# First feed-forward part in seven block products instead of eight, and the modulation rows moved from VectorE to GpSimd and ScalarE

## Chip, cores and metric

One core of a Trainium2 chip. The metric is the time on the device in microseconds, of one execution of the whole program; the median of three runs before the change is 2452.07 us (2451.47 to 2453.34).

## The reference

Two layers over 1024 latent tokens of width 1024. Layer 0 mixes tokens by attention, layer 1 by a short gated convolution, and each is followed by a SwiGLU feed-forward part with 2816 inner features. Every sub-layer is normalized, then scaled and shifted, and its result is gated, with six vectors a layer that come from silu(c) times `ada_w`:

```python
sh1, sc1, g1, sh2, sc2, g2 = jnp.split((silu_c @ ada_w[i] + ada_b[i])[:, None, :], 6, axis=-1)
...
x = x + g1 * y
x = x + g2 * swiglu(modulate(rmsnorm(x, norm_ffn[i]), sh2, sc2), ffn_w_gate[i], ffn_w_up[i], ffn_w_down[i])

def swiglu(h, w_gate, w_up, w_down):
    return (jax.nn.silu(h @ w_gate) * (h @ w_up)) @ w_down
```

All is float32. The output is the latent stream after a last RMSNorm.

## The kernel before

**Precision.** A float32 operand is held as two fp32r parts, a high one (`_hi`) that ScalarE rounds and a low one (`_lo`) that VectorE makes by subtraction. A product of two such operands is three matmuls (`mm3`: hi.hi, hi.lo, lo.hi; lines 571 to 573), each 128x128 by 128x512.

**Layout.** `x` and `h` lie transposed: 8 chunks of 128 features by 1024 tokens, the tokens in two halves A and B of 512. PSUM has 8 banks of 512: 0 to 3 for gate and up, 4 to 7 for the down product.

**Stages.** Prologue, attention, output projection, f0 (feed-forward of layer 0), the convolution, f1 (feed-forward of layer 1), last norm. Each engine's program is written out by hand in order; engines meet at semaphores (`wait_ge`, `then_inc`), and an instruction that waits holds all that stands behind it on its engine. SP issues all loads, in one queue.

**f0 before.** 11 blocks of 2x128 inner features (`ffn`, `inner`). A block is four units of gate and up (8 chunks x 2 x 3 = 48 matmuls each) and a down product for each half (8 x 2 x 3 = 48 each): 288 matmuls. Weight tiles (128x1024) go through `raw` and are split into `w_hi`, `w_lo`; `t_lo` counts tiles whose low part is made, and a tile's load waits until the tile two before it has been split. `to_x` adds a down bank, times the gate vector, to `x`; PE may fill the bank again once that is done (`bank_free`).

**Modulation rows before.** The 48 columns of layer 1's vectors are 48 rows of `ada_w`: each is loaded (128x1024, `modf_in`), multiplied by `row_f` (silu(c)) and summed along the row by one VectorE instruction (`mod_row_f`, L2256), five rows a block, from two buffers. `modf_c` counts them. After the last, `mods` and the scale vectors of layer 1 are made.

**f1 before.** Block 0 as in f0; the other ten (s = 0 to 9, `WINO`) by seven block products in place of eight. Both W^T and h are cut 2x2 (two tiles by two halves of the 8 chunks; two halves of the chunks by two halves of the tokens): A11, A12, A21, A22 of the weights, and sums S1 to S4; B11, B21, B22 and T1 to T4 of h, made once (`b_part`, `b_top`, `b_low`). A product has 4 chunks x 3 = 12 matmuls, 7 products for each of gate and up: 168, and 96 of the down products: 264 a block. Operands go through rings of four (`op_hi`, `op_lo`): ACT's `operand_top` n waits for product n - 4, VectorE's `operand_low` follows. VectorE adds the products up out of PSUM (`part`: C11, U2, U3, U5, C22, C21, C12); ACT takes silu of a corner's gate (`corner_gate`), VectorE multiplies (`corner_mult`), ACT rounds (`corner_split`), VectorE makes the low part (`corner_low`, counted by `gl`). The down product of half A runs one block late, behind products A11 and A12 of GATE; that of B later in the block. `quad_in` loads a block's four gate and up tiles into `rq`, line 747 its two down tiles into `w_lo_f`, copied by `down_top` and `down_low`.

**At the seams.** The norm of a half is: squares by ACT, sums by POOL (L2679), column sum by PE (`job_sum`), root by ACT (`job_sqrt`), reciprocal and diagonal by VectorE (`job_diag`), broadcast by PE (`job_bcast`), copy `rstd` by ACT (`job_out`). Then `h_scaled`, `h_top_of`, `h_low` make h chunk by chunk (`h_chunks`), with `to_x` of the other half between.

## Time and profile before

| | |
|---|---|
| median of three runs | 2452.07 us |
| the profiled execution | 2453.06 us, its span 2451.7 us |
| mean granted TensorE clock | 0.990 |
| PE busy | 2397.5 us (98%), 11229 matmuls |
| DVE, ACT, POOL busy | 1507.0, 711.8, 150.1 us |
| the chain that ended last | PE 93% of it, DVE 4% |

PE is TensorE's matmuls, PEld its weight loads, DVE VectorE, ACT ScalarE, POOL GpSimd, SP the queue that issues loads. Times are from the span's start. f0 lies between about 655 and 1385 us, the convolution up to 1746, f1 up to 2426. A matmul in the timeline has about 0.39 us because matmuls are pipelined; what counts is from start to start. "Idle before" is the time in which the engine did nothing, "releaser" what ended it. The granted clock is a share of 2.4 GHz.

### The profile page before, as it was taken

To read this page: it belongs to the slowest core of one execution; us is meant where nothing else is said; L and a number is where in the kernel's file an instruction comes from. 1 tells how busy PE (TensorE), PEld (TensorE's weight loads), DVE (VectorE), ACT (ScalarE), POOL (GpSimd) and SP (SyncE) were. 2 spreads that over 40 slices of the span, in tenths; PEclk is the share of its full clock that TensorE was granted. 3 is DMA by queue.
4 is the path that set the end of the run, shared out by engine and by line. 5 is a ranking of instruction groups with operands and counts; after the bars stand their busy time and mean duration, and the time that the engine had idled before them with its cause. 6 is when DMAs were issued, how large, how long until landed. Compare 5 with 4: busy or idle time off the path is not lost.

```text
span 2451.7 us, 28775 instructions
## 1 busy us (share of the span) xinstructions
PE 2397.5 (98%) x11229; PEld 1977.7 (81%) x11229; DVE 1507.0 (61%) x2204; ACT 711.8 (29%) x1105; POOL 150.1 (6%) x109
## 2 busy tenths in 40 slices
PE   7999999999999999999999999999999999999997
PEld 4878888888788888888888788888778888888886
DVE  4667777786665444454443763553887777777775
ACT  5345545553421111011111421111532222222223
POOL 0111121100300000000000300000300000000002
PEclk9999999999999999999999999999999999999998
DMA  7101111123222222222211111111101111111102
GB/s 285 33 24 42 50 49 41 41 78 116 91 95 79 93 86 86 95 89 83 93 63 51 59 53 32 64 44 42 52 9 53 59 52 52 52 52 56 56 27 86
DMA packets 48050, 163.31 MB, mean 67 GB/s; under 512 B 5184, under 2 KB 6592, under 8 KB 47808
## 3 DMA queue, kind: packets, MB, share of 16 engines
q1 hardware_dynamic: 47936, 161.72, 20.1%
q8 instruction: 80, 1.31, 0.2%
q14 instruction: 34, 0.28, 0.0%
HBM read 157.51 MB, written 4.19 MB: 66 GB/s over the span
## 4 chain that ended last, share of the span: by engine, by line
PE 93%; DVE 4%; ACT 1%; DMA 1%; issue 1%; POOL 0%; SPq 0%; ACTq 0%; DVEq 0%; POOLq 0%
PE ps L571 26%; PE ps L573 26%; PE ps L572 26%; PE ps L993 3%; PE ps L927 2%; PE ps L931 1%; PE ps L929 1%; PE ps L928 1%; PE ps L932 1%; PE ps L972 1%; PE ps L974 1%; PE ps L973 1%; DVE h_lo L2221 1%; DVE x L2000 1%; DMA ada_ring<-ada_pe 1%; PE ps L1015 1%
## 5 line engine op out<-in xcount | busy, mean ns | idle before, releaser
L571 PE MATMUL ps<-h_hi,w_hi 128*128 128x512 f32 x1152 | 451.7, 392 | 11.3 <-DVE h_lo L2221 11.2
L572 PE MATMUL ps<-h_lo,w_hi 128*128 128x512 f32 x1152 | 449.4, 390 | 0.0
L573 PE MATMUL ps<-h_hi,w_lo 128*128 128x512 f32 x1152 | 449.3, 390 | 0.0
L2000 DVE SCALAR_TENSOR_TENSOR x<-ps,mods,x 128x512 f32<-128x512 f32 x448 | 327.9, 748 | 140.0 <-PE ps L573 119.8
L571 PE MATMUL ps<-g_hi,w_hi 128*128 128x512 f32 x832 | 325.2, 391 | 3.4 <-DVE x L2000 1.8
L572 PE MATMUL ps<-g_lo,w_hi 128*128 128x512 f32 x832 | 323.8, 389 | 0.0
L573 PE MATMUL ps<-g_hi,w_lo 128*128 128x512 f32 x832 | 323.7, 389 | 0.0
L571 PEld LDWEIGHTS ps<-h_hi,w_hi 128*128 128x128 f32 x1152 | 216.9, 188 | 61.0 <-DVE h_lo L2221 16.6
L573 PEld LDWEIGHTS ps<-h_hi,w_lo 128*128 128x128 f32 x1152 | 217.0, 188 | 45.4
L572 PEld LDWEIGHTS ps<-h_lo,w_hi 128*128 128x128 f32 x1152 | 217.0, 188 | 44.4
L2241 DVE TENSOR_TENSOR ab<-ab,ps 128x512 f32<-128x512 f32 x48 | 33.0, 687 | 312.6 <-PE ps L573 307.5
L2679 POOL TENSOR_TENSOR acc<-acc,sq 128x512 f32<-128x512 f32 x52 | 75.4, 1450 | 1876.0 <-ACT sq L1324 1873.4
L571 PEld LDWEIGHTS ps<-g_hi,w_hi 128*128 128x128 f32 x832 | 156.2, 188 | 39.0 <-DVE x L2000 3.8
L573 PEld LDWEIGHTS ps<-g_hi,w_lo 128*128 128x128 f32 x832 | 156.2, 188 | 32.6
L572 PEld LDWEIGHTS ps<-g_lo,w_hi 128*128 128x128 f32 x832 | 156.2, 188 | 31.9
L1344 ACT CAST w_hi<-raw 128x1024 fp32r<-128x1024 f32 x112 | 113.6, 1050 | 197.4 <-PE ps L573 156.5
L1567 ACT ACTIVATE ab<-ps 128x512 f32<-128x512 f32 x48 | 28.7, 598 | 489.8 <-PE ps L573 489.7
L1854 DVE TENSOR_TENSOR pt_lo<-ps,pt_hi 128x512 fp32r<-128x512 f32 x160 | 110.1, 689 | 72.3 <-ACT pt_hi L1412 71.7
L1634 ACT CAST op_hi<-rq 128x512 fp32r<-128x512 f32 x120 | 73.5, 621 | 237.6 <-PE ps L573 236.4
L1854 DVE TENSOR_TENSOR w_lo<-raw,w_hi 128x1024 fp32r<-128x1024 f32 x108 | 131.0, 1229 | 16.5 <-ACT w_hi L1344 16.3
L1412 ACT CAST pt_hi<-ps 128x512 fp32r<-128x512 f32 x160 | 93.8, 587 | 131.6 <-PE ps L993 131.6
L571 PE MATMUL ps<-h_hi,op_hi 128*128 128x512 f32 x320 | 125.1, 391 | 2.0 <-DVE w_lo L1854 2.0
(336 smaller groups left out, 4030.4 us busy)
## 6 DMA issues: line engine op xcount, KB each, us to landing
raw<-stream SPq DMA_DIRECT2D x112, 512.0 KB, 3.6
mod_raw_f<-ada_rows SPq DMA_DIRECT2D x48, 512.0 KB, 3.7
rq<-stream SPq DMA_DIRECT2D x40, 512.0 KB, 3.5
mod_raw<-ada_rows SPq DMA_DIRECT2D x32, 512.0 KB, 3.5
w_lo_f<-stream SPq DMA_DIRECT2D x20, 512.0 KB, 4.0
ada_ring<-ada_pe SPq DMA_DIRECT2D x16, 512.0 KB, 11.0
x<-x_t SPq DMA_DIRECT2D x8, 512.0 KB, 7.2
out_t<-x SPq DMA_DIRECT2D x16, 256.0 KB, 2.1
```

Of the source, the lines that this page charges most:

```text
L571: nc.tensor.matmul(out, w[0][wi], a[0][ai], start=start, stop=False)
L572: nc.tensor.matmul(out, w[0][wi], a[1][ai], start=False, stop=False)
L573: return nc.tensor.matmul(out, w[1][wi], a[0][ai], start=False, stop=stop)
L927: nc.tensor.matmul(dst, qa[par][0][:, q], ckv_hi[:, k0:k1], start=True, stop=False)
L993: last = nc.tensor.transpose(ps[:, bank, j * P:(j + 1) * P], pbuf[:, 4 * (gb % 2) + j, k * P:(k + 1) * P], ident[:])
L1344: copy(dst, raw[k][:]).then_inc(t_hi, 1)
L1412: copy(pt_hi[:, (10 * gb + k) % 4, :], ps[:, bank, :]).then_inc(ra, 1)
L1634: copy(op_hi[:, at % 4, :], operand_a(s, mat, name)).then_inc(op_h, 1)
L1854: return nc.vector.tensor_tensor(dst, full, hi.bitcast(F32), ALU.subtract)
L2000: nc.vector.scalar_tensor_tensor(out=x[:, m, HALF[half]], in0=ps[:, out_bank(d, m), :], scalar=mods[:, gate + m:gate + m + 1], in1=x[:, m, ...
L2241: nc.vector.tensor_tensor(ab[unit % 2][:], ab[unit % 2][:], ps[:, 2 * (unit % 2) + 1, :], ALU.mult)\
L2679: nc.gpsimd.tensor_tensor(acc_of(j)[:, 0:cols], acc_of(j)[:, 0:cols], sq[C.n["sqa"] % 2][:, 0:cols], ALU.add).then_inc(sqa, 1)
```

## The change

- f0 runs as f1 does: block 0 as before, then ten blocks s = 0 to 9 of seven products; f1's are now s = 10 to 19. All helpers take s for both parts (`at_first`, `at_end`: first and tenth of a part).
- The last block of each part (`at_end`) has another order of products (A22 ahead of S1), and its own down products are cut in two (`down_end`): first the corner that is ready, then the other. The norm of half A (`job_sum`, `job_bcast`) comes before and inside the last down product.
- Corners are now put together in `g_full`, which shares the memory of `g_hi` and `g_lo`; so C11 and C22 are read after the last `to_x` of a down product and not before it. `ab` is free, and in f0 `mod_raw_f` lies there, one buffer.
- The modulation rows: SP loads a row when ACT has summed the one before it, POOL multiplies it by `row_f`, ACT sums it (`row_sum`). Blocks s = 0 to 5 of f0 take five rows, 6 to 8 take six. The scale vectors of layer 1 are made after block 8.
- The convolution's first tiles are loaded after f0's last block, and the start of the convolution stands in `conv_start`.

The rows' places, and SP (loads):

```diff
+ROWS_OF = {s: range(5 * s, 5 * s + 5) if s < 6 else range(6 * s - 6, 6 * s) for s in range(WINO - 1)}
...
-            if n >= 2:
-                sp.wait_ge(modf_c, n - 1)
-            sp.dma_start(mod_raw_f[n % 2][:], ada_rows[N_ATT_MOD + n]).then_inc(in_modf[n % 2], 16)
+            if n:
+                sp.wait_ge(modf_c, n)
+            else:
+                sp.wait_ge(gl, GL_F0 + 4)
+            sp.dma_start(mod_raw_f[:], ada_rows[N_ATT_MOD + n]).then_inc(in_modf, 16)
...
+        def down_in(s):
+
+            at = f0_at if s < WINO else f1_at
+            sp.wait_ge(dn, 8 * (down_at(s) + 2))
+            for f in range(2):
+                sp.dma_start(w_lo_f[:, 4 + f, :], stream[at(6 * (s % WINO + 1) + 4 + f)]).then_inc(in_dn[f], 16)
...
+        def wino_in(s):
+
+            rows = list(ROWS_OF.get(s, ()))
+            for n in rows[1:4]:
+            if at_end(s):
+                down_in(s)
+                return
+            for mat in (GATE, UP):
+                sp.wait_ge(op_l, product_n(s, mat, "A22") + 1)
+                quad_in(s + 1, mat, 1)
+            for n in rows[4:5]:
                 modf_in(n)
+            sp.wait_ge(op_l, product_n(s, GATE, "S4") + 1)
+            quad_in(s + 1, GATE, 0)
+            for n in rows[5:]:
+                modf_in(n)
+            down_in(s)
+            sp.wait_ge(op_l, product_n(s, UP, "S4") + 1)
+            quad_in(s + 1, UP, 0)
+            for n in ROWS_OF.get(s + 1, ())[:1]:
+                modf_in(n)
+
+        stream_in(12, 14)
+        sp.wait_ge(dn, 8 * D_F0)
+        sp.wait_ge(t_lo, 14)
+        quads_first(0)
+        modf_in(0)
+        for s in range(WINO):
+            wino_in(s)
+        sp.wait_ge(op_l, product_n(WINO - 1, GATE, "S4") + 1)
+        stream_in(14, len(TILES))
```

PE (products and the end of a part's last block):

```diff
+        def down_end(s, d, half, corners, norm_job=None):
+
+            for at, corner in enumerate(corners):
+                f = CORNER_F[corner]
+                pe.wait_ge(gl, corner_gl(s, corner))
+                for m in range(4):
+                    if at == 0:
+                        bank_free(d, m)
+                    last = mm3(ps[:, 4 + m, :], (w_hi, w_lo), (ALL, 4 + f, slice(m * P, (m + 1) * P)),
+                               (g_hi, g_lo), (ALL, f, HALF[half]), at == 0, at == 1)
+                    if at == 1:
+                        last.then_inc(dn, 1)
+                if at == 0 and norm_job is not None:
                     job_bcast(norm_job)
+            for m in range(4, KD):
+                bank_free(d, m)
+                for f in range(2):
+                    last = mm3(ps[:, 4 + m % 4, :], (w_hi, w_lo), (ALL, 4 + f, slice(m * P, (m + 1) * P)),
+                               (g_hi, g_lo), (ALL, f, HALF[half]), f == 0, f == 1)
+                last.then_inc(dn, 1)
...
+            products(s, (UP, "A11"), (UP, "A12"), (GATE, "S2"), (GATE, "S3"))
+            if at_end(s):
+                pe.wait_ge(gl, corner_gl(s - 1, "C12"))
+                down_of(d_was + 1, B)
+                products(s, (UP, "S2"), (UP, "S3"), (GATE, "A22"), (UP, "A22"), (GATE, "S1"))
+                pe.wait_ge(dn_l, 2 * s + 2)
+                down_end(s, d_was + 2, A, ("C11", "C21"))
+                products(s, (UP, "S1"), (GATE, "S4"))
+                job_sum(job_a)
+                products(s, (UP, "S4"))
+                down_end(s, d_was + 3, B, ("C22", "C12"), job_a)
+                return
+            products(s, (UP, "S2"), (UP, "S3"), (GATE, "S1"))
+            if not at_first(s):
```

ACT:

```diff
+        def row_sum(s, n):
+
+            for row in ROWS_OF.get(s, ())[n:n + 1]:
+                act.wait_ge(modf_p, row + 1)
+                nc.scalar.activation(mod_raw_f[:], mod_raw_f[:], ACT.Identity,
+                                     accum_out=mods[:, 48 + row:49 + row]).then_inc(modf_c, 1)
...
+                return
+            row_sum(s, 1)
+            for n in range(8, 11):
                 operand_top(s, n)
+            row_sum(s, 2)
+            operand_top(s, 11)
+            operand_top(s, 12)
+            row_sum(s, 3)
             corner_gate(s, "C22")
             operand_top(s, 13)
             corner_split(s, "C22")
-            if s < WINO - 1:
-                operand_top(s + 1, 0)
+            operand_top(s + 1, 0)
+            row_sum(s, 4)
             corner_gate(s, "C21")
             for f in range(2):
                 down_top(s, f)
             corner_split(s, "C21")
-            if s < WINO - 1:
-                operand_top(s + 1, 1)
+            operand_top(s + 1, 1)
+            row_sum(s, 5)
             corner_gate(s, "C12")
+        def wino_end(s, jobs_a):
+
+            for n in range(8, 12):
+                operand_top(s, n)
...
+            corner_gate(s, "C21")
+            operand_top(s, 12)
+            corner_split(s, "C21")
+            operand_top(s, 13)
+            corner_gate(s, "C22")
+            for m in range(KD):
+                squares_of(jobs_a, down_at(s) + 2, m)
+            corner_split(s, "C22")
+            corner_gate(s, "C12")
+            job_sqrt(jobs_a)
+            if s < WINO:
+                top("conv", 0, "c", 0, (prod, product_n(s, UP, "S2") + 1))
+                top("conv", 0, "x", 0, (prod, product_n(s, UP, "S2") + 1))
+            corner_split(s, "C12")
+            job_out(jobs_a)
...
+        def conv_start(turn, jobs_b):
+
+            d = down_at(WINO - 1) + 3
+            free = (prod, product_n(WINO - 1, UP, "S1") + 1)
+            top("conv", 0, "b", 0, free)
+            for k in range(KD):
+                h_top_of(turn, A, k)
+                if k >= 2:
+                    squares_of(jobs_b, d, k - 2)
+            for m in (6, 7):
+                squares_of(jobs_b, d, m)
+            for name in "cxb":
+                top("conv", 0, name, 1, free)
```

VectorE (the reads of C11 and C22 move behind the updates of x), and POOL:

```diff
-            part(s, "C11", GATE)
             for m in range(4):
                 to_x(d_was, m, gate)
...
             for m in range(4, KD):
                 to_x(d_was, m, gate)
...
+            part(s, "C11", GATE)
...
+            for s in range(s0, s0 + WINO):
+                wino_block(s, gate, job_a)
+                if s == WINO - 2:
+                    dve.wait_ge(modf_c, N_F0_MOD)
+                    own(nc.vector.tensor_tensor(mods[:, 48:96], mods[:, 48:96], adab[:, 48:96], ALU.add))
+                    scale_vec(3, mods[:, mod_col(1, SCALE1):mod_col(1, SCALE1) + KD], 2).then_inc(sv_set, 1)
+                    scale_vec(4, mods[:, mod_col(1, SCALE2):mod_col(1, SCALE2) + KD], 3).then_inc(sv_set, 1)
+
+        def conv_start(turn, gate):
+
+            d = down_at(WINO - 1) + 3
+            dve.wait_ge(sv_set, 3)
+            for f, name in ((0, "c"), (0, "x")):
+                low("conv", 0, name, f)
+            for k in range(KD):
+                h_chunks(turn, A, k, k + 1)
+                to_x(d, k, gate)
+                if k == 0:
+                    low("conv", 0, "b", 0)
+            for name in "cxb":
+                low("conv", 0, name, 1)
...
         squares_sum(J_MIX)
         squares_sum(J_MIX + 1)
+        pool.wait_ge(silu_done, 3)
+        for n in range(N_F0_MOD):
+            pool.wait_ge(in_modf, 16 * (n + 1))
+            nc.gpsimd.tensor_tensor(mod_raw_f[:], mod_raw_f[:], row_f[:], ALU.mult).then_inc(modf_p, 1)
```

## Rows read from the trace of the kernel before

**Rows 1.** Busy time of each engine over the span (the page's first part)
```profile
PE 2397.5 (98%) x11229; PEld 1977.7 (81%) x11229; DVE 1507.0 (61%) x2204; ACT 711.8 (29%) x1105; POOL 150.1 (6%) x109
```

**Rows 2.** Windows of the span (start:end, length, each engine's busy us (instructions), clock, DMA)
```profile
1086.22:1151.50 65.28, 65.28 (x289) 54.07 (x288) 31.14 (x44) 8.40 (x11) 0.00 (x0) 1.00 0.28 89
2049.14:2109.00 59.86, 59.86 (x266) 49.56 (x265) 42.41 (x63) 16.32 (x27) 0.00 (x0) 1.00 0.17 53
1869.63:2389.14 519.51, 519.51 (x2293) 430.18 (x2292) 365.77 (x536) 137.91 (x221) 0.00 (x0) 1.00 0.15 49
```

**Rows 3.** Waits over the whole span (engine line <- waited for: total us, times, longest)
```profile
PE ps L571 <- DVE h_lo L2221: 11.2, 9, 2.0
PE ps L1299 <- POOL acc L2679: 3.8, 1, 3.8
```

**Rows 4.** What touches mod_raw_f (durations min/median/max in ns), and where its loads land
```profile
L2256 DVE SCALAR_TENSOR_TENSOR mod_raw_f<-mod_raw_f,row_f x48: 1215/1218/1226, 705.3 to 1274.4; 128x1024 f32<-128x1024 f32 x48
DMA to landing us min/median/max: 3.3/3.7/4.9
```

**Rows 5.** The adds of line L2679 (durations min/median/max in ns)
```profile
L2679 POOL TENSOR_TENSOR acc<-acc,sq x52: 1277/1303/2381, 630.9 to 2428.7; 128x512 f32<-128x512 f32 x52
```

**Rows 6.** Groups by shape on ACT (busy us, mean ns | idle before)
```profile
L1449 ACT ACTIVATION_READ_ACCUMULATOR pbuf<-ps,nmax 128x1 f32 x64 | 12.7, 198 | 0.0
```

**Rows 7.** Timeline around a block of f1 (start, length, ..., [idle before <- releaser])
```profile
2051.64 1.40 DVE L2000 SCALAR_TENSOR_TENSOR x<-ps,mods,x 128x512 f32<-128x512 f32 x2
...
2090.14 0.80 SPq L747 DMA_DIRECT2D w_lo_f<-stream  x2
2095.64 0.62 ACT L1634 CAST op_hi<-rq 128x512 fp32r<-128x512 f32 x1 [0.70 <-PE ps L573]
2097.47 1.99 ACT L1663 CAST w_hi<-w_lo_f 128x1024 fp32r<-128x1024 f32 x2
2101.38 1.22 DVE L1854 TENSOR_TENSOR w_lo<-w_lo_f,w_hi 128x1024 fp32r<-128x1024 f32 x1
2103.11 0.68 DVE L2409 TENSOR_TENSOR ab<-part_ug,ps 128x512 f32<-128x512 f32 x1
```

**Rows 8.** Timeline of POOL and DVE where the convolution begins
```profile
1383.51 4.08 POOL L2679 TENSOR_TENSOR acc<-acc,sq 128x512 f32<-128x512 f32 x2 [16.92 <-ACT sq L1324]
...
1383.99 0.75 DVE L2221 SCALAR_TENSOR_TENSOR h_lo<-tmp,mods,h_hi 128x512 fp32r<-128x512 f32 x1
1384.65 0.75 DVE L2000 SCALAR_TENSOR_TENSOR x<-ps,mods,x 128x512 f32<-128x512 f32 x1
1386.36 1.78 DVE L2221 SCALAR_TENSOR_TENSOR h_lo<-tmp,mods,h_hi 128x512 fp32r<-128x512 f32 x1
1388.06 0.74 DVE L2000 SCALAR_TENSOR_TENSOR x<-ps,mods,x 128x512 f32<-128x512 f32 x1
```

**Rows 9.** Line L747, the loads of down tiles in f1
```profile
DMA to landing us min/median/max: 3.4/4.0/4.7
```

**Rows 10.** Timeline of PE, matmuls with idle time before them
```profile
721.61 0.50 PE L571 MATMUL ps<-g_hi,w_hi 128*128 128x512 f32 x1 [0.69 <-DVE x L2000]
...
1393.54 0.80 PE L571 MATMUL ps<-h_hi,w_hi 128*128 128x512 f32 x1 [2.03 <-DVE h_lo L2221]
...
1752.89 0.50 PE L571 MATMUL ps<-h_hi,w_hi 128*128 128x512 f32 x1 [1.71 <-DVE h_lo L2221]
...
1805.12 0.47 PE L571 MATMUL ps<-g_hi,w_hi 128*128 128x512 f32 x1 [1.10 <-issue]
...
1826.44 0.47 PE L571 MATMUL ps<-h_hi,op_hi 128*128 128x512 f32 x1 [2.02 <-DVE w_lo L1854]
```

**Rows 11.** A window in f1's first product block
```profile
1826.80:1830.20 3.40, 3.40 (x10) 2.62 (x9) 3.40 (x6) 0.00 (x0) 0.00 (x0) 0.50 0.01 2
```

**Rows 12.** Timeline of PE behind its last wide matmul
```profile
2430.30 1.30 PE L1299 MATMUL ps<-ones,acc 128*128 128x1 f32 x8 [3.75 <-POOL acc L2679]
2431.46 3.55 PE L1299 MATMUL ps<-ones,tmp 128*128 128x1 f32 x16
```

590 lines of the change are left out of this document (239 added, 351 removed).

## The prediction, as it stood before the change was run

> **What bounds the kernel now.** I read the page first: TensorE (PE) is busy 2397.5 of 2451.7 us, VectorE (DVE) 61%, ScalarE (ACT) 29%, GpSimd (POOL) 6% [rows 1]. Then the busy time by windows: a block of the first feed-forward part (f0) takes 65.28 us and a seven-product block of the second part (f1) 59.86 us, both with PE busy in every microsecond and the clock at 1.00 (2.4 GHz) [rows 2]. f0 has 288 matmuls of 512 columns in a block and f1 264 (the counts in the rows take in one or two at the edges), so both run at 65.28/288 = 59.86/264 = 0.2267 us each. So the matmul count sets the time, and anything else costs only where PE stands still. The waits of PE over the whole span are few: 11.2 us for h_lo (the three places where a part begins) and 3.8 us for POOL at the end [rows 3]. So I ask of each step of the change: does PE wait for it?
>
> **The change, part by part.**
>
> 1. Fewer matmuls. In ten blocks of f0 gate and up take 2 x 7 products x 4 x 3 = 168 instead of 192. 240 x 0.2267 = 54.4 us less. All of it is on the path.
>
> 2. The 48 multiply-and-sum steps (1.22 us each, 58 us with their accumulator reads left out) leave DVE [rows 4]. The f1 block has 42.4 us of DVE work in 59.86 us [rows 2], none of it late, and f0 now gets the same. Worth nothing by itself.
>
> 3. Each of the 48 rows is now one chain on a single buffer: SP loads it from HBM, POOL multiplies 128x1024, ACT sums it, SP loads the next. No row shows the multiply. POOL's adds of 128x512 have a median of 1.30 us and a maximum of 2.38 [rows 5], so it lies between 1.3 and 4.8; I take 2 x 1.30 = 2.6, since both inputs double. ACT: 0.20 us for the accumulator [rows 6] plus 1.05 for 1024 elements (two such copies, overlapping a little, take 1.99 [rows 7]) = 1.25. A row's load takes 3.7 us [rows 4]. A chain is then 3.7 + 2.6 + 1.25 + about 0.3 = 7.9 us, and five or six of them (39 or 47 us) fit in a block. In the middle of a block this hides: ACT works 16.3 us of a block's 59.86 [rows 2], and operands are copied three products (8 us) ahead.
>
> 4. What POOL does to DVE. While POOL adds, DVE operations with two SBUF inputs wait for it: h_lo (L2221) takes 0.75 us in one place and 1.78 in another, and the update of x (L2000), with one input in PSUM, stays at 0.74 [rows 8]. So one 2.6 us multiply can hold DVE for 2.6 us. By the Trainium skill (SBUF — State Buffer, Who interferes with whom) such an instruction and a GpSimd one that reads SBUF take turns and the second blocks fully; the trace agrees with 1.78 against 0.75 us [rows 8]. By the rule the whole 2.6 us of a multiply counts, as in my sum; if only the 1.03 us seen here were ever held, steps 4 to 6 would come to some 6 us less.
>
>    Where is DVE's critical stretch? At the end of a block DVE must finish the low parts of C21, of the second down tile and of an operand before it reads C12 (2103.11 to 2103.79), which frees the bank that product A12 of the next block wants 2.72 us after the block starts at 2103.56, at 2106.28 [rows 7]: 2.5 us of cover. For blocks 0 to 5 the fifth row's sum falls behind the operand copy at 2095.64, so the next block's first row is loaded from 2097.6, lands at 2101.2 and is multiplied until 2104. It holds DVE by about 2.6 us: PE waits 0.1 to 0.2 us. 6 x 0.2 = 1.2 us (0 to 6).
>
> 5. The sixth row in blocks 6, 7 and 8. SP issues it *before* the two down tiles, and its load waits for the fifth sum. Now the down tiles go out at 2090.14 [rows 7]; then they go at about 2098.0 and 2098.4, behind the row's load. A load lands 3.5 us after its issue, and one right behind another up to 4.7 [rows 9], some 1.3 us more each. They land at 2102.5 and 2103.8. ACT, which copies them in its queue ahead of the C21 cast and the operand, is through at 2104.8 instead of 2099.5, C21's cast at 2105.4, then DVE: low of C21 2106.1, of the tile 2107.3, of the operand 2107.9, C12 2108.5. PE starts A12 at 2108.7 instead of 2106.3: 2.4 us. DVE is now 5.4 us late. Its first update of x (2051.64 to 2052.4) ends 2.2 us before the fifth down group wants its bank (2049.14 + 5.44 = 2054.6) [rows 7], and 2.8 once the C11 read (0.6) stands behind the updates; 5.4 - 2.4 - 2.8 = 0.2 us more. And the next row's multiply (blocks 6, 7) or the late scale vectors (block 8, 0.81 + 1.37 us) lie in that same stretch: some 2.2 more. 4.8 us at each of three places, 14.4. Idle of 2.02 and 2.03 us was followed by slower matmuls (starts 0.43 us apart) at a granted clock of 0.50 (1.2 GHz), idle of 1.71 us was not [rows 10, 11]; 3.4 us at half clock cost some 1.5, and I add 2.4 for three places at half odds. Together 16.8 (0 to 25).
>
> 6. First product block. In f1 it loses 5.9 us against 0.2267 a matmul: 1.1 and its edge at the first down product, 2.0 and its edge for the low part w_lo, some 1.4 for the clock at 0.50 behind that [rows 10, 11], small waits for the rest. f0 gets the same. DVE's C11 read now stands behind all updates of x, so the chain to that low part is 0.6 longer in both parts, and in f0 row 1's multiply (loaded after the sum of row 0, on POOL some 22 us into the block) lands in DVE's sums: 2.6. f0: +9.1 (6 to 11), f1: +0.6. An old wait of 0.69 us in f0's first block goes, 1.0 with its edges [rows 10].
>
> 7. The seam to the convolution. Now it loses 11.3 us against the pitch from 1347.3 to 1401 (waits for h_lo, the last of them 2.0 us, and the half clock behind it [rows 10]). In the new order the A half's norm is done before the last down product, which helps; but tile b of the convolution can only be loaded when DVE has made the low part of tile c (some 1.2 us after the last corner), and ACT copies b *ahead* of the first h_hi. Its load (3.6 us) and copy (1.05) put h_hi about 6 us behind the last corner's low part; DVE's queue has the updates of x behind h_lo, and PE's fifth down group waits for the first of them some 5 us. Then DVE's pace of 2.0 us a chunk, 3.4 once POOL adds (from 1384.65 to 1388.06), sets the end, as now [rows 8]. I work out 14.0 us lost, 15.5 with the clock. +4.2 (1 to 8).
>
> 8. The end. Now the A half's rstd comes so late (job_bcast at m = 5) that the squares of B wait; PE starts the last sums after 3.75 us of idleness, and most of the 40 run at half clock, 16 in 3.55 us, the last until 2438.4 [rows 12]. In the new order A's rstd is there before, the sums start about 0.3 us behind the last matmul, and most run at half of those 0.22 us. 7.35 us by the steps, 6.5 with some at half clock (3 to 7.4).
>
> Sum: -54.4 - 1.0 + 9.1 + 0.6 + 1.2 + 16.8 + 4.2 - 6.5 = -30.0 us. The profiled execution took 2453.06 us (span 2451.7 and 1.4 around it), 1.0 above the median of the three runs. 2453.06 - 30.0 - 1.0 = **2422.1 us**.
>
> **The rivals.**
>
> *Covered after all* (33%): the rows cost nothing, because POOL's multiply is nearer 1.3 us or falls between DVE's instructions, and the down tiles land in time. For: only 2.5 us decide at each place, and DVE idles 17 us in a block [rows 2]. Against: SP's order is fixed, and the sixth row's load stands ahead of the down tiles whatever POOL takes. -30.0 - 2.6 - 1.2 - 16.8 = -50.6: 2401.5 us, up to 2412 if half the price stays.
>
> *Every row hurts* (10%): multiplies of up to 4.8 us (twice POOL's longest add) overrun the 2.5 us of cover at all nine places, with a clock fall at each: 2 to 3 us more at six places, and the upper ends of steps 6 and 7. 2436 to 2445 us.
>
> *Slower than before* (3%): the chain of rows sets the pace. ACT stands at a row's sum until POOL is done, and operand copies stand behind it. With a multiply of x us the 48 rows take 48 (5.25 + x). Nine blocks have 9 x 59.86 = 539 us, and 30 + 18 us are left until the gain is gone (18 being steps 4 and 5, which this replaces): 48 (5.25 + x) = 587, so from x = 7.0 us the kernel is slower; at 8 us it takes 48 x 13.25 = 636, some 2501 us. Nothing in the rows is near: 4.8 is the most.
>
> *The change doesn't bring its matmuls* (4%): f0's products wait throughout for operands, so that a block takes 65 us as before: about 2451 us. Against it: f1 does the same work from the same buffers with no gap in nine blocks [rows 2].
>
> **How the numbers follow.** The forecast (2412 to 2435) has 50%, and it gives the time. With the rivals' ends, about a tenth left out on either side: 2399 to 2436. A measurement of this kernel can tell 0.2% (4.9 us) from no change. Faster by more: all but the slower rival and the last: 93%. Within: 4%. Slower: 3%.
>
> **What the profile will show.** Step 1: 11229 - 240 = 10989 matmuls, f0 blocks of 59.86 us without gaps in blocks 1 to 4. Step 3: 48 POOL multiplies of about 2.6 us. Steps 4 and 5: DVE two-input operations of 2 to 3 us beside them; PE gaps at the beginnings of blocks 7, 8 and 9, each for DVE, with down tiles issued some 8 us later than in blocks 0 to 5. Step 6: a gap of about 5 us in f0's first product block. Step 7: PE waits of some 5 us for x in the last down product of f0, h_hi behind the copy of tile b. Step 8: the last sums right behind the last matmul, some 18.5 us from there to the end. The prediction is wrong if blocks 7 to 9 begin without gaps (then near 2404), or if POOL takes far more than 2.6 us.

## The result, and the profile after

| | before | after |
|---|---|---|
| median of the runs | 2451.99 us (2451.47 to 2453.34, 4 runs) | 2416.55 us (2413.85 to 2417.92, 4 runs) |
| the profiled execution, its span | 2453.06, 2451.7 us | 2413.85, 2412.3 us |
| ratio of the runs | | 0.9853, 95% interval 0.9836 to 0.987 |

The change saves 35.4 us; 30 were forecast, and 2416.55 lies inside the range of 2399 to 2436. The profiled execution is the fastest of its four, 2.7 us under their median, while that of before is 1.1 over its own; so the two traces differ by 39.4 us of span, and that is what is accounted for below.

The page of the changed kernel, busy time of each engine (compare [rows 1]): 240 matmuls fewer, DVE up from 61% to 69%, since f0 now has f1's sums to make, and ACT and POOL up with the rows.

```profile
PE 2344.8 (97%) x10989; PEld 1932.8 (80%) x10989; DVE 1663.6 (69%) x2399; ACT 849.7 (35%) x1371; POOL 275.0 (11%) x157
```

Windows (start:end, length, busy us of PE, PEld, DVE, ACT, POOL with instructions, clock, DMA). The first is f0's second product block: 59.88 us where a block took 65.28 [rows 2], PE busy throughout. The second is the eighth, which has six modulation rows as the one ahead of it has: 4.4 us longer, with the gap of 2.50 us at its end and the clock down at its start.

```profile
775.45:835.33 59.88, 59.88 (x266) 49.57 (x265) 44.36 (x63) 21.51 (x38) 12.84 (x5) 1.00 0.29 97
1136.90:1201.20 64.30, 61.80 (x265) 50.53 (x265) 44.38 (x63) 22.63 (x39) 14.84 (x6) 0.97 0.29 98
```

Waits of PE between 1290 and 1680 us, the seam from f0 to the convolution (engine line <- waited for: total us, times, longest), where the larger waits of before were for h_lo [rows 3]:

```profile
PE ps L605 <- DVE x L2069: 6.1, 4, 5.4
PE ps L605 <- DVE h_lo L2290: 2.8, 2, 2.0
```

The 48 multiplies (durations min/median/max in ns, first and last start): 2.40 us each (2.6 was taken). ACT's sum has a median of 1.06 us and 0.185 for the accumulator (1.25 was taken).

```profile
L2780 POOL TENSOR_TENSOR mod_raw_f<-mod_raw_f,row_f x48: 2390/2403/5727, 714.5 to 1257.2; 128x1024 f32<-128x1024 f32 x48
```

**Where block 7 ends and block 8 begins.** Timeline of SP, ACT, DVE and PE. SP issues the sixth row at 1189.11 and the down tiles right behind it (in the experiment that turns the two round, the tiles go at 1181.64); they land for ACT at 1194.5 and 1195.9. DVE's low parts follow, and its read of C12 at 1199.97 lets PE go at 1200.70, 2.50 us late. Then the multiply of the next block's first row starts, and DVE's subtraction of two SBUF inputs beside it takes 2.86 us, where 0.69 is usual. DVE's updates of x come at 1209.75, just in time.

```profile
1189.11 0.33 SPq L736 DMA_DIRECT2D mod_raw_f<-ada_rows  x1
1189.48 1.95 SPq L766 DMA_DIRECT2D w_lo_f<-stream  x2
1194.52 1.05 ACT L1677 CAST w_hi<-w_lo_f 128x1024 fp32r<-128x1024 f32 x1 [4.91 <-DMA w_lo_f<-stream]
1195.95 1.05 ACT L1677 CAST w_hi<-w_lo_f 128x1024 fp32r<-128x1024 f32 x1 [0.37 <-DMA w_lo_f<-stream]
1199.97 0.68 DVE L2399 TENSOR_TENSOR g_full<-part_ug,ps 128x512 f32<-128x512 f32 x1
1200.70 0.50 PE L605 MATMUL ps<-h_hi,op_hi 128*128 128x512 f32 x1 [2.50 <-DVE g_full L2399]
1202.66 2.88 POOL L2780 TENSOR_TENSOR mod_raw_f<-mod_raw_f,row_f 128x1024 f32<-128x1024 f32 x1 [6.97 <-DMA mod_raw_f<-ada_rows]
1203.23 2.86 DVE L2349 TENSOR_TENSOR op_full<-rq 128x512 f32<-128x512 f32 x1
1209.75 2.72 DVE L2069 SCALAR_TENSOR_TENSOR x<-ps,mods,x 128x512 f32<-128x512 f32 x4
```

**f0's first product block.** Row 1's multiply (725.05) lies in DVE's sums. DVE's subtraction at 728.56 takes 2.77 us, all behind it is 2.1 us late, and PE waits 4.69 us for the low part of T3.

```profile
725.05 5.73 POOL L2780 TENSOR_TENSOR mod_raw_f<-mod_raw_f,row_f 128x1024 f32<-128x1024 f32 x1 [8.11 <-DMA mod_raw_f<-ada_rows]
728.56 2.77 DVE L2351 TENSOR_TENSOR rq<-rq,op_full 128x512 f32<-128x512 f32 x1
735.00 0.77 PE L605 MATMUL ps<-h_hi,op_hi 128*128 128x512 f32 x1 [4.69 <-DVE w_lo L1923]
```

**The seam.** ACT waits 4.34 us for tile b, copies it, and only then rounds the first h_hi; DVE's first update of x stands behind that, and PE waits 5.38 us for it.

```profile
1342.26 1.04 ACT L1404 CAST w_hi<-raw 128x1024 fp32r<-128x1024 f32 x1 [4.34 <-DMA raw<-stream]
1343.21 1.33 ACT L1619 ACTIVATE h_hi<-tmp,mods 128x512 fp32r<-128x512 f32 x2
1344.62 0.74 DVE L2069 SCALAR_TENSOR_TENSOR x<-ps,mods,x 128x512 f32<-128x512 f32 x1
1345.42 0.79 PE L605 MATMUL ps<-g_hi,w_hi 128*128 128x512 f32 x1 [5.38 <-DVE x L2069]
```

**The end.** The last sums start with no idle time behind the last wide matmul, where PE stood 3.75 us before, and 16 take 1.93 us instead of 3.55 [rows 12].

```profile
2394.87 0.95 PE L1359 MATMUL ps<-ones,acc 128*128 128x1 f32 x8
2395.68 1.93 PE L1359 MATMUL ps<-ones,tmp 128*128 128x1 f32 x16
```

### The profile page after: what moved, and what is told of

Its sections match the earlier page's. It is cut to its first block, busy times and chain, and to the rows that moved or that the text cites. A ratio compares the mean times of both kernels' runs of the same rounds, so it can differ in the third digit from the quotient of the medians.

```text
span 2412.3 us, 29109 instructions
## 1 busy us (share of the span) xinstructions
PE 2344.8 (97%) x10989; PEld 1932.8 (80%) x10989; DVE 1663.6 (69%) x2399; ACT 849.7 (35%) x1371; POOL 275.0 (11%) x157
## 4 chain that ended last, share of the span: by engine, by line
PE 90%; DVE 6%; DMA 2%; ACT 1%; issue 1%; SPq 0%; POOL 0%; DVEq 0%; ACTq 0%; POOLq 0%
PE ps L605 25%; PE ps L607 25%; PE ps L606 24%; PE ps L1052 3%; PE ps L986 2%; PE ps L990 1%; PE ps L988 1%; PE ps L987 1%; PE ps L991 1%; PE ps L1031 1%; PE ps L1032 1%; PE ps L1033 1%; DVE x L2069 1%; DVE h_lo L2290 1%; DVE w_lo L1923 1%
## 5 line engine op out<-in xcount | busy, mean ns | idle before, releaser
L605 PE MATMUL ps<-h_hi,op_hi 128*128 128x512 f32 x640 | 252.3, 394 | 13.5 <-DVE w_lo L1923 7.3
L607 PE MATMUL ps<-h_hi,op_lo 128*128 128x512 f32 x640 | 251.6, 393 | 0.0
L605 PE MATMUL ps<-h_hi,w_hi 128*128 128x512 f32 x512 | 202.0, 395 | 10.2 <-DVE h_lo L2290 10.2
L606 PE MATMUL ps<-h_lo,w_hi 128*128 128x512 f32 x512 | 200.2, 391 | 0.0
L607 PE MATMUL ps<-h_hi,w_lo 128*128 128x512 f32 x512 | 200.1, 391 | 0.0
L606 PE MATMUL ps<-h_lo,op_hi 128*128 128x512 f32 x480 | 188.2, 392 | 0.0
L606 PE MATMUL ps<-w_lo,op_hi 128*128 128x512 f32 x480 | 188.1, 392 | 0.0
L2780 POOL TENSOR_TENSOR mod_raw_f<-mod_raw_f,row_f 128x1024 f32<-128x1024 f32 x48 | 126.1, 2628 | 470.0 <-DMA mod_raw_f<-ada_rows 470.0
L1923 DVE TENSOR_TENSOR op_lo<-rq,op_hi 128x512 fp32r<-128x512 f32 x240 | 177.0, 745 | 1.2
L607 PEld LDWEIGHTS ps<-h_hi,op_lo 128*128 128x128 f32 x640 | 121.6, 190 | 25.6
```

The source lines that it names most:

```text
L605: nc.tensor.matmul(out, w[0][wi], a[0][ai], start=start, stop=False)
L606: nc.tensor.matmul(out, w[0][wi], a[1][ai], start=False, stop=False)
L607: return nc.tensor.matmul(out, w[1][wi], a[0][ai], start=False, stop=stop)
L1923: return nc.vector.tensor_tensor(dst, full, hi.bitcast(F32), ALU.subtract)
L2780: nc.gpsimd.tensor_tensor(mod_raw_f[:], mod_raw_f[:], row_f[:], ALU.mult).then_inc(modf_p, 1)
```

## The experiments

A measure that serves for most of them: how many matmuls PE starts between 765 and 1300 us, where f0's product blocks run. At the pitch (the time from one matmul's start to the next) of 0.2267 us it is 2360 to 2362. The changed kernel has 2315, so it loses some 47 x 0.2267 = 10.6 us there, at three places: where blocks 7, 8 and 9 begin (gaps of 1.85, 2.50 and 1.89 us). The window rows of that stretch (start:end, length, PE busy us (matmuls), clock, DMA), in this order: the changed kernel (the run beside the experiments), e1_down_first, e2_mul_short, e4_no_rows, e5_sum_early, e6_all, e9_late_first, e10_mid_first. The text takes them up one by one.

```profile
765.00:1300.00 535.00, 528.89 (x2315) 0.99 0.27 91
765.00:1300.00 535.00, 532.53 (x2347) 1.00 0.27 93
765.00:1300.00 535.00, 528.10 (x2321) 1.00 0.26 92
765.00:1300.00 535.00, 535.00 (x2362) 1.00 0.15 51
765.00:1300.00 535.00, 534.08 (x2356) 1.00 0.27 93
765.00:1300.00 535.00, 527.62 (x2320) 1.00 0.28 96
765.00:1300.00 535.00, 531.95 (x2340) 1.00 0.29 97
765.00:1300.00 535.00, 534.93 (x2360) 1.00 0.29 97
```

### The changed kernel once more (after_again)

> The changed kernel as it is, for comparison on the same chip. About 2416.5 us, with the losses at the same places: 4.7 us of gap in the first product block, 1.9, 2.5 and 1.9 us where blocks 7, 8 and 9 begin, 5.4 us at the seam.

2415.59 us (2410.99 to 2417.33), ratio 0.9853 (0.9836 to 0.9869). Same places, same gaps within 0.5 us. Its runs differ by up to 6 us, so the medians of the experiments below are good to some 2 us, and the places are told apart by their traces.

### Down tiles ahead of the sixth row (e1_down_first)

```diff
-            for n in rows[5:]:
-                modf_in(n)
             down_in(s)
+            for n in rows[5:]:
+                modf_in(n)
```

> The changed kernel, with one thing turned round: in blocks 6, 7 and 8 the load of the sixth modulation row is issued behind the two down tiles, and not ahead of them. The rows' own times stay (the sixth load still waits for the fifth sum, the next block's first row for the sixth), so GpSimd multiplies where it did. Theory 1 (order of loads): the changed kernel loses 3.8, 4.5 and 2.2 us where blocks 7, 8 and 9 begin, because the down tiles wait behind the row's load; turned round they are issued some 8 us earlier, the three gaps (1.85, 2.50, 1.89 us) and the two falls of the clock go, and the kernel takes 10.5 us less: about 2406 us against 2416.5. Theory 2 (the multiply holds VectorE): the multiplies lie where they lay, VectorE's low parts still wait for them, the gaps stay at half or more, and the time falls by less than 5 us: 2412 to 2416.

2407.81 us (2406.01 to 2410.24), ratio 0.9818 (0.9802 to 0.9835): 8 to 9 us less. 2347 matmuls: 3.3 us of the 10.6 are left. The gaps for the C12 read are gone. The down tiles are issued at 1181.64 now. What is left are two gaps of 1.19 and 1.29 us at another place, the fifth down group (the fifth of a down product's eight chunks, the first that needs a bank to be free again), and there the multiplies are to be seen. Timeline of the same boundary: the sixth row's multiply holds an operand's low part for 2.89 us, the next one the low part of C12 for 2.88 us, and PE waits for the update of x behind them.

```profile
1193.19 3.16 POOL L2780 TENSOR_TENSOR mod_raw_f<-mod_raw_f,row_f 128x1024 f32<-128x1024 f32 x1 [12.52 <-DMA mod_raw_f<-ada_rows]
1194.01 2.89 DVE L1923 TENSOR_TENSOR op_lo<-rq,op_hi 128x512 fp32r<-128x512 f32 x1
1201.04 2.70 POOL L2780 TENSOR_TENSOR mod_raw_f<-mod_raw_f,row_f 128x1024 f32<-128x1024 f32 x1 [4.69 <-DMA mod_raw_f<-ada_rows]
1201.41 2.88 DVE L1923 TENSOR_TENSOR g_lo<-g_full,g_hi 128x512 fp32r<-128x512 f32 x1
1207.42 0.50 PE L605 MATMUL ps<-g_hi,w_hi 128*128 128x512 f32 x1 [1.29 <-DVE x L2069]
```

So theory 1 holds for 7.3 of 10.6 us, and theory 2 names the rest.

### A short multiply (e2_mul_short)

```diff
-            nc.gpsimd.tensor_tensor(mod_raw_f[:], mod_raw_f[:], row_f[:], ALU.mult)
+            nc.gpsimd.tensor_tensor(mod_raw_f[:, 0:128], mod_raw_f[:, 0:128], row_f[:, 0:128], ALU.mult)
```

> The changed kernel, with GpSimd's 48 multiplies cut to 128 of 1024 columns (the rest of a row is left unmultiplied, so the vectors of layer 1 are not the real ones). A multiply falls from 2.40 us to about 0.3 to 0.5. Theory 1 (order of loads): the losses where blocks 7, 8 and 9 begin stay at 10.5 us together, since the sixth row's load waits for ScalarE, which sums the fifth row late in its own queue and not because GpSimd is late; only the first product block gains, its gap falls from 4.69 to 2.6 us (one multiply of 2.1 us less in VectorE's way). In all 2 to 3 us less: about 2414. Theory 2 (the multiply holds VectorE): the gaps at the three blocks go as well, 10.5 + 2.1 = 12.6 us less: about 2404.

2410.69 us (2410.41 to 2412.11), ratio 0.9831 (0.9815 to 0.9848). The median of a multiply is 0.46 us. The three boundary gaps stay, at 1.91, 2.92 and 2.08 us (2321 matmuls), so the multiply is not what makes them; the first product block's gap falls from 4.69 to 2.76 us. The places agree with theory 1. The median fell by 5 to 6 us where these places give 2.9 against the pitch; the rest is not accounted for.

### No rows at all (e4_no_rows)

```diff
         def row_sum(s, n):
-            for row in ROWS_OF.get(s, ())[n:n + 1]:
+            for row in ():
```

(and the same for their loads, multiplies and the waits for them.)

> The changed kernel without the 48 modulation rows in the first feed-forward part: no loads, no multiplies, no sums (the vectors of layer 1 are then not the real ones). Theory 1: the rows cost what is lost where blocks 7, 8 and 9 begin (10.5 us) and some 2.1 us in the first product block, and nothing else: about 12.6 us less, 2404 us; blocks 0 to 5 as they are. Theory 2 (every row costs a little that the losses against the matmuls' pitch don't show, through the clock or through ports): 20 us less or more, under 2397. Theory 3 (the stalls have another cause, the new order of VectorE's reads): under 5 us less, and the gaps stay.

2402.22 us (2400.77 to 2403.97), ratio 0.9794 (0.9778 to 0.9811): 13 to 14 us less. 2362 matmuls, every block at the pitch, and 2.61 us of gap in the first product block. Theory 1: the rows cost 10.6 us at three boundaries and some 2 us in the first block, nothing elsewhere.

### The fifth sum earlier (e5_sum_early)

```diff
             row_sum(s, 3)
+            row_sum(s, 4)
             corner_gate(s, "C22")
...
             operand_top(s + 1, 0)
-            row_sum(s, 4)
+            row_sum(s, 5)
             corner_gate(s, "C21")
...
             operand_top(s + 1, 1)
-            row_sum(s, 5)
```

> The changed kernel, with SP's order as it was, but ScalarE sums the fifth row of every block ahead of corner C22's gate, and the sixth behind the next block's first operand copy, one place earlier each. In the changed kernel the fifth row was multiplied by 1180.8 us in block 7 and summed only at 1187.9, because the sum stood behind the split of C22; ScalarE was idle for 8.4 us in between. Theory 1 (the losses where blocks 7, 8 and 9 begin come from the late sum, through the load that waits for it and the down tiles behind that load, and from the multiply, which then falls into VectorE's last stretch of the block): the sixth row is loaded at 1182, the down tiles 0.9 us later than without it, the multiply ends at 1188 and both gaps go, the one for the down tiles and the one that stayed when only the loads were turned round (1.2 and 1.3 us, 3.2 with their clock): about 10 us less, 2406. Theory 2 (six rows a block are too many for VectorE whatever their place): 3 us or more stay of the 10.5, 2409 or more.

2405.85 us (2403.43 to 2408.44), ratio 0.9812 (0.9795 to 0.9828): 10 us less. 2356 matmuls; one gap of 0.92 us is left of the three. Theory 1 on the whole; why one stays is seen in the next.

### Three cures at once (e6_all)

```diff
+ROWS_OF = {s: range(6 * s - 6, 6 * s) for s in range(1, WINO - 1)}
...
         quads_first(0)
-        modf_in(0)
```

(with the sums of e5_sum_early and the tiles of e3_seam, which follows.)

> The changed kernel with three things at once: the sums one place earlier, as in e5_sum_early; no row in block 0, six in each of blocks 1 to 8; and the convolution's first tiles split earlier, as in e3_seam. If the three costs stand side by side, their gains add: 10 us where blocks 7 to 9 begin, 2.1 us in the first product block (its gap falls from 4.69 to 2.6 us, as it did without any rows), 3 to 3.6 us at the seam: about 15.5 us less than the changed kernel, 2401 us. If six rows a block are too many, blocks 2 to 9 now all begin with a loss of 1 to 3 us, and the time is 2408 or more.

2406.62 us (2405.16 to 2408.52), ratio 0.9812 (0.9796 to 0.9828): no better than e5_sum_early alone. The gains in the first block (gap 2.61 us) and at the seam came, but blocks 2 to 8 each began with 0.9 to 1.2 us of gap, 2320 matmuls. The second theory, then, but is it the number? Timeline of the start of block 8: the multiply is that of the *next* block's first row, loaded once the sixth is summed, and it holds the operand's low part that stands right ahead of the C12 read.

```profile
1196.90 3.10 POOL L2781 TENSOR_TENSOR mod_raw_f<-mod_raw_f,row_f 128x1024 f32<-128x1024 f32 x1 [6.79 <-DMA mod_raw_f<-ada_rows]
1197.67 2.88 DVE L1922 TENSOR_TENSOR op_lo<-rq,op_hi 128x512 fp32r<-128x512 f32 x1
1201.20 0.50 PE L605 MATMUL ps<-h_hi,op_hi 128*128 128x512 f32 x1 [1.18 <-DVE g_full L2398]
```

Once in e5_sum_early that row's load was slow (issued at 1188.47, multiplied from 1194.19), and the multiply held only the product behind the reads, at 1195.27, for 1.88 us; PE didn't wait.

### The first row later, and in between (e9_late_first, e10_mid_first)

Both have all of e6_all and e8_more. The wait that e9_late_first adds to SP:

```diff
             for n in ROWS_OF.get(s + 1, ())[:1]:
+                sp.wait_ge(op_l, product_n(s + 1, GATE, "A12") + 1)
                 modf_in(n)
```

> As e8_more, with one wait more on SP: a block's first row is loaded only when VectorE has made the low part of the next block's second operand. In e6_all and e8_more blocks 2 to 8 each began with a gap of 0.9 to 1.2 us (7 to 9 us in all), and there the multiply of the next block's first row started 56.2 to 56.9 us into the block (counted from ScalarE's first copy of a block), across VectorE's last reads; where it started at 53.4 to 55 (five rows) or 58.2, nothing was lost. Theory 1 (its place decides, not the number of rows): the load goes out at about 56, the multiply starts at 59.5, behind the reads; the gaps go: 8 us less than e8_more, about 2394.5. Theory 2: the multiply then holds the low part of C12 and the next sums of operands, as at the blocks after the sixth row in the changed kernel (2.9 us on op_full), and PE waits there instead: 0 to 3 us less.

2399.52 us (2398.16 to 2400.39), ratio 0.9781 (0.9764 to 0.9797): 3 us less than e8_more (below). 2340 matmuls. The boundary gaps became gaps of 0.3 to 0.6 us at the fifth down group: the multiply holds a sum, and the updates of x behind it are late. Theory 2.

```profile
1197.16 2.55 POOL L2781 TENSOR_TENSOR mod_raw_f<-mod_raw_f,row_f 128x1024 f32<-128x1024 f32 x1 [11.81 <-DMA mod_raw_f<-ada_rows]
1197.48 2.77 DVE L2351 TENSOR_TENSOR rq<-rq,op_full 128x512 f32<-128x512 f32 x1
1203.98 0.50 PE L605 MATMUL ps<-g_hi,w_hi 128*128 128x512 f32 x1 [0.52 <-DVE x L2069]
```

The wait that e10_mid_first has in its place:

```diff
+                sp.wait_ge(corner_full, corner_n(s, "C21"))
```

> As e9_late_first, but SP loads the next block's first row once VectorE has multiplied corner C21, some 3 us earlier. In e9_late_first its multiply started 61.5 us into the block, held the sums of operands (2.77 us for one) and made the first update of x late by 0.3 to 0.6 us at seven places, 5.0 us lost with their edges; in e6_all and e8_more it started at 56.2 to 56.9 and held the reads, 9.2 to 9.5 us lost. Once, in e5_sum_early, it started at 58.2, held only the product behind the reads (1.88 us) and nothing was lost. Theory 1 (a window between the reads and the sums is free): the load goes out at about 54.7, the multiply starts at 58 to 58.3, no gaps in blocks 2 to 9, 4 to 5 us less than e9_late_first: about 2395. Theory 2 (wherever it starts, VectorE is late by the same 2 us): gaps of 0.3 to 0.6 us stay, 2399.

2395.37 us (2390.84 to 2399.37, 5 runs), ratio 0.9761 (0.9748 to 0.9774): better than either kernel by 57 and 21 us. 2360 matmuls: all the 48 rows, six in a block, at no cost. The multiply starts right behind the reads and holds only the product of C12, which nobody needs soon. The profiled execution is the slowest of the five, but not for the rows: in this stretch it runs at the pitch.

```profile
1191.88 2.41 POOL L2781 TENSOR_TENSOR mod_raw_f<-mod_raw_f,row_f 128x1024 f32<-128x1024 f32 x1 [8.96 <-DMA mod_raw_f<-ada_rows]
1192.51 2.32 DVE L2407 TENSOR_TENSOR g_full<-g_full,g_full 128x512 f32<-128x512 f32 x1 [0.17 <-ACT g_full L1659]
```

Counted from ScalarE's first copy of a block (its `part_ug` out of PSUM, 0.5 us behind PE's first matmul of the block; 59.84 us apart where nothing is lost), the same 2.4 us multiply cost 9 us over the part when it started some 3 us (2.9 to 3.6 in e6_all) ahead of that copy's undisturbed place, nothing at 2 us ahead (1.7 to 2.1, once 1.0), and 5 us when it started mostly 1.7 us behind it. Some 5 us ahead of it, where blocks 0 to 5 of the changed kernel have it, it cost nothing either.

### The seam (e3_seam, e8_more)

```diff
                 squares_of(jobs_a, down_at(s) + 2, m)
+            if s < WINO:
+                top("conv", 0, "c", 0, (prod, product_n(s, UP, "S2") + 1))
+                top("conv", 0, "x", 0, (prod, product_n(s, UP, "S2") + 1))
             corner_split(s, "C22")
...
             corner_low(s, "C22")
+            if s < WINO:
+                low("conv", 0, "c", 0)
```

(and the low part of x behind corner C12's product; both go from their old places.)

> The changed kernel, with the first two convolution tiles (c and x) copied by ScalarE ahead of the split of corner C22 and their low parts made by VectorE between the last corners, and not behind the last one. Tile b's load waits for tile c's low part, so it goes out some 5 us earlier. Theory 1 (the copy of tile b stands ahead of the first h_hi): in the changed kernel h_hi waits 4.34 us for tile b's load, and PE waits 5.38 us for the first update of x. Now b has landed when the norm's copy is done (1337.9 in the changed kernel's time); h_hi comes at about 1339.0 instead of 1343.2, the first update of x is done at 1341.1 instead of 1345.4, PE's wait falls to 1 us, the clock doesn't fall there, and the seam loses 4.3 to 5.5 us less: about 2411.5. Theory 2 (VectorE's own pace of 2 us a chunk sets the seam's end): the first wait goes, but PE then waits as long for the later chunks; 0 to 2 us less.

2412.90 us (2410.21 to 2414.41), ratio 0.9841 (0.9824 to 0.9857): some 3 us less than the changed kernel (2.7 and 3.7 against its two medians). The first h_hi comes 1.5 us after the copy of rstd (1335.95) instead of 5.9, and PE's 5.38 us of wait fall to 0.92. But 1.46 us come back at the next update, behind tile b's low part, and PE reaches the broadcast earlier and waits 2.72 us for its diagonal instead of 1.22.

```profile
1337.43 1.39 ACT L1619 ACTIVATE h_hi<-tmp,mods 128x512 fp32r<-128x512 f32 x2
1339.65 0.50 PE L605 MATMUL ps<-g_hi,w_hi 128*128 128x512 f32 x1 [0.92 <-DVE x L2069]
1342.77 0.50 PE L605 MATMUL ps<-g_hi,w_hi 128*128 128x512 f32 x1 [1.46 <-DVE x L2069]
1373.42 1.16 PE L864 MATMUL ps<-diag,ones 128*128 128x128 f32 x8 [2.72 <-DVE diag L1932]
```

The stretch from 1290 to 1680 us (before, changed, e3_seam, e8_more):

```profile
1290.00:1680.00 390.00, 384.35 (x1687) 0.99 0.16 50
1290.00:1680.00 390.00, 379.88 (x1667) 0.99 0.15 52
1290.00:1680.00 390.00, 381.44 (x1680) 1.00 0.16 52
1290.00:1680.00 390.00, 385.51 (x1699) 1.00 0.16 53
```

The change lost 20 x 0.2267 = 4.5 us there, e3_seam won 2.9 back. Mostly theory 1, and part of it moved on, as theory 2 has it. e8_more adds to e6_all:

```diff
-                if k == 0:
-                    low("conv", 0, "b", 0)
+            low("conv", 0, "b", 0)
...
-                        if first and e == 3 and k == 1:
+                        if first and e == 3 and k == 4:
```

> As e6_all, with two more moves at the convolution's start: VectorE makes tile b's low part behind all eight chunks and not behind the first, and PE broadcasts the norm of half B three chunks later in the fourth tile. In e3_seam PE waited 1.46 us for the second update of x, which stood behind that low part, and 2.7 us at the broadcast for the diagonal. Theory 1: both waits were PE's own and go, 1.2 + 2.5 us less than e6_all. Theory 2: VectorE has the same work up to the last chunk's low part, so the 1.2 us only move to the later waits for h_lo, and only the broadcast's 2.5 us go.

2402.74 us (2400.15 to 2402.80), ratio 0.9795 (0.9778 to 0.9811): 3.9 us less than e6_all. The 1.46 us went (0.32 is left) without the later waits for h_lo growing (2.03 and 0.23 us here, 2.04 and 0.72 in e6_all): theory 1 in that. The broadcast's 2.5 us were not there to win: e6_all waits 1.19 us at it, and not 2.72 as e3_seam does, and e8_more 0.32. The whole stretch gains 2.9 us over e6_all (1699 matmuls against 1686). The two profiled executions also differ by 2.4 us at the end, where e6_all ran most of the last sums at a granted clock of 0.50 and e8_more at 1.00, and that is no work of the edit.

### The end (e7_tail)

```diff
-                if at == 0 and norm_job is not None:
+                if at == 0 and norm_job is not None and s < WINO:
                     job_bcast(norm_job)
...
+                if m == 5 and norm_job is not None and s >= WINO:
+                    job_bcast(norm_job)
```

> The changed kernel, with one thing put back in the second part only: PE broadcasts the norm of half A behind chunk 5 of the last down product, as in the kernel before, and not between its two corners. Theory 1 (the early norm shortens the end): the copy of rstd is then done about 1.7 us before the last wide matmul ends and not 7.4 us before, the squares of half B stand behind it, PE is idle for some 3.7 us ahead of the last sums, and from the last wide matmul to the end it takes 25 us again instead of 17.4: 7 to 8 us more than the changed kernel, about 2423. Theory 2 (the end is shorter only because the clock happened to stand at 1.00 there): 0 to 2 us more.

2425.38 us (2423.98 to 2427.66), ratio 0.9886 (0.987 to 0.9903): 9 to 10 us more. The old end is back: idle 3.75 us, 16 sums in 3.55, and 25.7 us from the last wide matmul's start to the end, where the kernel before takes 25.5 and the changed one 17.6. The end gives 8.1 us of the difference; f0, which is the same program, lost 3.2 us more in this execution by chance. Theory 1 in the main. Theory 2 has a part: in e6_all, which has the early norm but the clock at 0.50 in most of the last sums, the end takes 20.0 us, and 20.5 in e10_mid_first; in the other traces with it 17.6 to 18.9.

```profile
2403.44 1.43 PE L1361 MATMUL ps<-ones,acc 128*128 128x1 f32 x8 [3.75 <-POOL acc L2731]
2404.72 3.55 PE L1361 MATMUL ps<-ones,tmp 128*128 128x1 f32 x16
```

This trace shows by chance what the prediction's fifth step had in mind (2307 matmuls, 8 fewer than the changed kernel); it is taken up below, under step 5.

### The kernel before, without its rows (b1_before_no_rows)

```diff
         def mod_row_f(n):
-            dve.wait_ge(in_modf[n % 2], 16 * (n // 2 + 1))
...
+            return
```

> The kernel before, without the 48 modulation rows in the first feed-forward part (no loads, no multiply-and-sum steps; the vectors of layer 1 are then not the real ones). Theory 1: VectorE did these 58 us of work beside PE's, and taking them away is worth nothing: within 1 us of 2452. Theory 2: with their loads and their time on VectorE they were late somewhere: 2 us less or more, and then part of the change's gain would come from moving them.

2450.51 us (2448.87 to 2453.69, 10 runs) against 2453.11, ratio 0.9991 (0.9981 to 1.0). The medians differ by 2.6 us, the ratio says 0 to 4.7, and the two theories were set at less than 1 and at 2 or more, so the times alone don't decide. The traces do for the most part. The wait of 0.69 us in f0's first block [rows 10] is gone, 1.0 us with its edges, the other waits differ by 0.5 us at most, and where f0 ran at the pitch before it does so here. Most of the rest of the difference lies in f1's first product block, where there were no rows: PE waits 2.02 us there before and 2.01 here, but the clock behind it is at 0.50 before [rows 11] and at 1.00 here. So of the 58 us of DVE's work all but 1 us were hidden.

## Why the prediction was right, and where it was off

What the traces show against its terms, in us of span:

| step | predicted | measured | where it is read |
|---|---|---|---|
| 1, matmuls | -54.4 | -54.4 | 10989 of them; blocks of 59.88 us |
| 6, f0's first block, with the old wait | +9.1 - 1.0 | +8.3 - 1.0 | gaps of 4.69, 1.11 and 0.41, and a clock fall |
| 6, f1's first block | +0.6 | +0.6 | its gap is 2.61 us, 2.02 before [rows 10] |
| 4, ends of blocks 0 to 5 | +1.2 | 0 | no gaps |
| 5, starts of blocks 7 to 9 | +16.8 | +10.6 | 2315 matmuls against 2362 |
| 7, the seam | +4.2 | +4.5 | 1667 against 1687 |
| 8, the end | -6.5 | -7.9 | 17.6 us from the last wide matmul's start, 25.5 before |
| sum | -30.0 | -39.3 | span 2412.3 against 2451.7 |

**Steps 1 and 2** held as worked out. That the rows' work on DVE was worth nothing, but for the old wait that step 6 has, is shown by b1_before_no_rows.

**Step 3** held to 0.2 us in its durations: 2.40 us for the multiply (2.6 taken), 1.24 for the sum (1.25), 3.5 for the load (3.7).

**Step 5** is where the sum was off, by 6.2 us. Its mechanism is shown: with the loads turned round the gaps of 1.85, 2.50 and 1.89 us go, with the fifth sum earlier they go but for one of 0.92, and with a short multiply they stay. The first stall was put at 2.4 us each, and it came at 2.1 on average (6.2 in all); the clock was put at 2.4 us for the three, and its two falls with the edges of the gaps took the other 4.4. What did not come was the other half, the 2.2 to 2.4 us for the fifth down group at each place. The step added a fall of the clock and a second stall for the same places, and they exclude each other: at 1.2 GHz PE reaches the fifth group later, and DVE has caught up. Four traces have this f0 (the changed kernel's two, e3_seam and e7_tail), so there are eight starts of blocks 7 and 8. In all eight DVE's first update of x is done 9.8 us behind PE's first matmul of the block. In seven the clock fell, and PE came to the fifth group 9.9 us behind it and didn't wait; in one, block 7 of e7_tail, the clock happened to stay up, PE came earlier, waited 1.41 us and went on at 9.9 us as well. At block 9 of the changed kernel, with neither, it is 8.3. Windows right behind the gap (length, busy, clock), first of the changed kernel, then of e7_tail, and e7_tail's timeline:

```profile
1137.20:1140.60 3.40, 3.40 (x10) 2.62 (x9) 3.40 (x4) 1.92 (x4) 2.19 (x1) 0.50 0.15 57
...
1138.70:1142.10 3.40, 3.40 (x16) 2.80 (x15) 3.23 (x5) 2.45 (x5) 1.49 (x1) 1.00 0.24 89
...
1140.92 2.89 DVE L2351 TENSOR_TENSOR op_full<-rq 128x512 f32<-128x512 f32 x1
1148.26 0.50 PE L605 MATMUL ps<-g_hi,w_hi 128*128 128x512 f32 x1 [1.41 <-DVE x L2071]
```

The second stall was sized too large as well, at 2.4 us; the one that came was 1.41, and 1.19 and 1.29 in e1_down_first. At block 9, where no row of a next block is multiplied, there was none, without a fall of the clock; the late scale vectors, for which the step had also put 2.2 us, took DVE 0.4 us there.

**Step 4** asked whether the next block's first row holds DVE in its last stretch. Behind blocks 0 to 5 nothing is lost; its multiply starts 4.7 to 5.4 us before ScalarE's first copy of the next block there, and what it holds is ready again in time. e6_all, e9_late_first and e10_mid_first show how narrow that is: the forecast of 0 to 6 us was right as a range. DVE's two-input operations of 0.69 us took 2.77 to 2.89 us beside a multiply of 2.40, so 2.1 to 2.2 of its 2.40 us counted where DVE met it at its start, and not the 1.03 us that the rows of before showed. That agrees with the rule of the Trainium skill (SBUF — State Buffer, SBUF: two separate sides), by which the first of the two keeps the shared ports for its whole instruction and the other fully blocks.

**Step 6** held: e4_no_rows and e6_all put the multiply's share of the first block at 2.1 us (gap 4.69 against 2.61).

**Step 7** held in size and in mechanism: e3_seam takes away the copy of tile b ahead of h_hi, and 4.5 us of wait go at that place. **Step 8** held in mechanism (e7_tail); it was 1.4 us small, since all the 40 sums ran at the full rate in the profiled execution, 16 in 1.93 us (3.55 in [rows 12]). That was chance as well: by the ends of 17.6 to 20.5 us above, the step is worth 5.0 to 7.9 us, and 6.5 lies within.

The rival "covered after all" did not come: the changed kernel still loses 10.6 us. Of the conditions that it named, the multiply's length does not decide: e2_mul_short has a multiply of 0.46 us and keeps the boundary gaps. That the down tiles land in time does, and the multiply's place. With the orders on SP and ACT changed it comes about, as e10_mid_first shows. "Every row hurts" did not come either (blocks 0 to 5 begin without gaps).

## What to carry to other kernels

Work that is moved to an idle engine costs by its place: ask which loads its queue then stands ahead of, and which instructions of the busy engine it meets. Look for what holds an early link of the chain (here a sum that ACT made 7 us after the multiply was done), since everything behind it then falls at the wrong time; one place earlier for it was worth 10 us, and a wait that puts a transfer, and so its multiply, some 1.5 us later another 7 (e8_more against e10_mid_first). When several costs are added up for one place, ask if one gives time back to the other.

## What the runs showed of the hardware

- A GpSimd multiply also waits for VectorE. With 128 columns its median is 0.46 us and its longest 3.73, at 724.15 us; with 1024 columns 2.40 and 5.73, at 725.05. Both stood beside a row of VectorE instructions that followed one another without idle time (in the changed kernel 724.43, 726.63, 727.23 and 727.83), and VectorE was held only at 728.56. In e10_mid_first, with no row in that block, the longest of the 48 is 2.57 us. By the Trainium skill (SBUF — State Buffer, Who interferes with whom) the order of issue decides who blocks. This trace agrees only in part: by its record, whose times are rough for GpSimd, the three VectorE instructions from 726.63 on started behind the multiply and still were not held.

```profile
L2780 POOL TENSOR_TENSOR mod_raw_f<-mod_raw_f,row_f x48: 457/462/3731, 713.5 to 1253.1; 128x128 f32<-128x128 f32 x48
```

- The update of x, with one input in PSUM, stayed at 0.73 to 0.75 us in every kernel, each of the 448 of a trace, as in [rows 8].
- Equal gaps of PE are followed by a fall of the clock in one execution and not in another: 2.02 us in f1's first product block of the kernel before, with a fall, and 2.01 us there in b1_before_no_rows, without; at block 7 1.85 us in the changed kernel, with, and 1.76 us in e7_tail, without. So the pattern that the prediction's step 5 took from [rows 10, 11], a fall behind 2.02 us and none behind 1.71, is not a limit. The same gaps then cost different time: between the two later gaps of f1's first product block (2.61 and 0.42 us) PE takes 26.8 us in the changed kernel and 25.2 in after_again. That is a part of why the runs of one kernel differ by up to 8.5 us here (e10_mid_first; 1.7 to 6.3 in the others), and those of the kernel before by 1.9 to 3.2.
